# Gains of two norms: multiplied into the activations, or into the weights that follow them

## The reference, cut to what matters

```python
def rms_norm(x, g):
    y = x * rsqrt(mean(x * x, axis=-1) + 1e-6)
    return y * g                        # g: one gain per channel (1024)

xn = rms_norm(x, norm_mix[0])
x = x + moba_attention(xn, w_qkv, w_o)  # qkv = xn @ w_qkv, w_qkv 1024 x 3072
x = x + squared_relu_mlp(rms_norm(x, norm_mlp[0]), ...)
xn = rms_norm(x, norm_mix[1])
# group g of 256 channels: (trailing mean over 2, 4, 8 or 16 positions of xn) - xn,
# then a 256 x 256 map per group, then a scale per output channel
x = x + einsum(pooled, pool_w) * pool_scale
```

## Time and profile before

| | us |
|---|---|
| median of 3 runs (lowest to highest) | 1084.13 (1082.69 to 1084.5) |
| the profiled execution's own time | 1084.07 |
| its span, first to last instruction | 1082.1 |
| TensorE busy in the span | 1069.3 |
| VectorE busy | 740.3 |
| ScalarE busy | 561.1 |

### The profile page before, as it was taken

One profiled execution on the slowest core, in us unless ns is written; L12 is line 12 of the kernel. 1 busy time (PEld: TensorE's weight loads), 2 busy tenths in 40 slices (PEclk: granted clock), 3 DMA queues, 4 the chain that ended last, 5 costly groups with the idle time before them and its releaser, 6 DMA issues.

```text
span 1082.1 us, 15294 instructions
## 1 busy us (share of the span) xinstructions
PE 1069.3 (99%) x5812; PEld 909.6 (84%) x5812; DVE 740.3 (68%) x1044; ACT 561.1 (52%) x723; POOL 40.4 (4%) x60
## 2 busy tenths in 40 slices
PE   9999999999999999999999999999999999999997
PEld 6888888888888888889888888888889778888886
DVE  5756675655786656558897966666897879666665
ACT  5556443434455435346675554445654766444453
POOL 1000000000000000000000220000300300000000
PEclk9999999999999999999999999999999999999999
DMA  9953266465447465546633665657576324754651
GB/s 332 336 173 111 87 217 216 166 205 182 159 140 257 159 214 171 202 137 169 210 118 105 213 204 177 196 181 245 151 245 225 91 79 157 232 185 164 203 185 39
DMA packets 127163, 195.84 MB, mean 181 GB/s; under 512 B 6977, under 2 KB 97217, under 8 KB 126994
## 3 DMA queue, kind: packets, MB, share of 16 engines
q1 hardware_dynamic: 123904, 185.77, 51.7%
q0 software_dynamic: 3216, 9.51, 3.1%
q10 hardware_dynamic: 2, 0.00, 0.0%
HBM read 194.21 MB, written 1.05 MB: 180 GB/s over the span
## 4 chain that ended last, share of the span: by engine, by line
PE 94%; DVE 3%; ACT 1%; issue 1%; DMA 0%; DVEq 0%; ACTq 0%
PE ps L2108 26%; PE ps L2007 15%; PE ps L2009 15%; PE ps L2008 15%; PE ps L2111 13%; PE ps L2190 2%; PE ps L2229 1%; PE ps L2049 1%; PE ps L2192 1%; PE ps L2255 1%; PE ps L2640 1%; DVE act L1244 1%; PE ps L2288 1%; DVE wlo L1119 1%; PE ps L2469 0%
## 5 line engine op out<-in xcount | busy, mean ns | idle before, releaser
L2108 PE MATMUL ps<-act,whi 128*128 128x512 f32 x1200 | 425.0, 397 | 0.1
L1119 DVE TENSOR_TENSOR wlo<-raw,whi 128x2048 fp32r<-128x2048 f32 (+2 forms) x161 | 364.0, 2277 | 87.8 <-ACT whi L678 87.3
L2111 PE MATMUL ps<-act,wlo 128*128 128x256 f32 x1200 | 336.6, 281 | 0.0
L678 ACT ACTIVATE whi<-raw 128x2048 fp32r<-128x2048 f32 (+2 forms) x170 | 317.4, 1887 | 26.5 <-PE ps L2009 21.5
L2108 PEld LDWEIGHTS ps<-act,whi 128*128 128x128 f32 x1200 | 225.3, 188 | 54.4 <-issue 0.2
L2111 PEld LDWEIGHTS ps<-act,wlo 128*128 128x128 f32 x1200 | 226.7, 189 | 2.0
L2009 PE MATMUL ps<-whi,hlo 128*128 128x512 f32 x400 | 157.3, 393 | 0.0
L2008 PE MATMUL ps<-wlo,hhi 128*128 128x512 f32 x400 | 156.7, 392 | 0.0
L2007 PE MATMUL ps<-whi,hhi 128*128 128x512 f32 x400 | 156.2, 391 | 0.1
L2007 PE MATMUL ps<-whi,act 128*128 128x512 f32 (+2 forms) x286 | 112.4, 393 | 1.2 <-DVE act L1819 0.6
L2009 PE MATMUL ps<-whi,act 128*128 128x512 f32 (+2 forms) x286 | 108.0, 377 | 0.0
(11 more groups left out here) (231 smaller groups left out, 1155.6 us busy)
## 6 DMA issues: line engine op xcount, KB each, us to landing
raw<-mlp_w_up_in SPq DMA_DIRECT2D x32, 1024.0 KB, 6.2
raw<-mlp_w_down_in SPq DMA_DIRECT2D x32, 1024.0 KB, 4.9
raw<-ffn_w_gate_in SPq DMA_DIRECT2D x22, 1024.0 KB, 5.3
raw<-ffn_w_up_in SPq DMA_DIRECT2D x22, 1024.0 KB, 5.4
raw<-ffn_w_down_in SPq DMA_DIRECT2D x22, 1024.0 KB, 4.8
raw<-attn_w_qkv_in SPq DMA_DIRECT2D x10, 1024.0 KB, 8.9
raw<-w_kv_shared_in SPq DMA_DIRECT2D x8, 1024.0 KB, 5.3
raw<-attn_w_o_in SPq DMA_DIRECT2D x4, 1024.0 KB, 5.1
```

The source lines that it names most:

```text
L678: nc.scalar.activation(whi[:, s, 0:width], raw[:, s, 0:width], ACT.Copy).then_inc(hi_ready, 1)
L1119: nc.vector.tensor_tensor(wlo[:, s, 0:width], raw[:, s, 0:width], whi[:, s, 0:width].bitcast(F32), ALU.subtract).then_inc(lo_ready, 1)
L2108: nc.tensor.matmul(bank(b + f), lhsT=w[0][:, at:at + P], rhs=act[:, k, :, :].rearrange("p a t -> p (a t)"), start=k == 0, stop=False, skip ...
L2111: ins = nc.tensor.matmul(bank(b + f, 0, T), lhsT=w[1][:, at:at + P], rhs=act_hi[:, k, :], start=False, stop=k == KT - 1, skip_group_check= ...
```

## The change

The gains of both norms are loaded as 16 rows of 128 values (8 KB), turned once by TensorE to one column per block k, and copied to a small tile `gains`. `whi` and `wlo` of chunks 0 to 11 are made in four pieces of 512 columns, each with the column of its block as a per-partition scale. `pool_scale` and the second gain are multiplied into the pooling's weights in eight pieces of 256 columns. x itself is turned at the start, and x itself is multiplied by the band. `first_gained`, the spreading of the row, and `gained("mix1", ...)` are gone. The first quarter's dummies are six instead of three. Two rows leave the list `ROWS`, the order on VectorE at the start is another, and TensorE waits for x (`x_loaded`, `x_rest_loaded`, `x_ready`) where it waited for `xs_ready`.

```diff
-ROWS = ["mix0", "mlp0", "mix1", "pool_scale", "mlp1", "final", ...
+ROWS = ["mlp0", "pool_scale", "mlp1", "final", ...
@@ ScalarE
+            def hi_gained(s, k, gain):
+                return nc.scalar.activation(whi[:, s, k * HALF:(k + 1) * HALF], raw[:, s, k * HALF:(k + 1) * HALF],
+                                            ACT.Copy, scale=gains[:, gain:gain + 1])
             def hi_part(s, width, loaded, freed, gain=None):
...
+                for k in range(4):
+                    ins = hi_gained(s, k, gain + k)
+                ins.then_inc(hi_ready, 1)
...
-            act.dma_start(rows[0:1, 0, :], row_source["mix0"]...).then_inc(first_row_loaded, 16)
+            act.dma_start(junk[0:2 * KT, 0:P], a["norm_mix"].rearrange("l (k p) -> (l k) p", p=P))\
+               .then_inc(gains_loaded, 16)
             def hi_part_of(c, h, landed, done):
                 act.wait_ge(landed, 16)
-                nc.scalar.activation(whi[... h * D:(h + 1) * D], raw[...], ACT.Copy).then_inc(done, 1)
+                for k in (2 * h, 2 * h + 1):
+                    ins = hi_gained(SLOT[c], k, 4 * c + k)
+                ins.then_inc(done, 1)
             copy_turned("mix0", (0,))
+            act.wait_ge(gains_ready, 1)
             hi_part_of(0, 0, first_half_loaded, first_half_hi)
@@ VectorE
+            def lo_gained(s, k, gain):
+                cols = slice(k * HALF, (k + 1) * HALF)
+                return nc.vector.scalar_tensor_tensor(out=wlo[:, s, cols], in0=raw[:, s, cols],
+                                                      scalar=gains[:, gain:gain + 1],
+                                                      in1=whi[:, s, cols].bitcast(F32), op0=ALU.mult, op1=ALU.subtract)
...
-            dve.wait_ge(first_row_spread, 1)
+            dve.wait_ge(gains_turned, 1)
+            nc.vector.tensor_copy(gains[:, :], bank(3, 0, 2 * KT)).then_inc(gains_ready, 1)
             dve.wait_ge(x_loaded, 16)
             dve.sem_inc(x_ready, 2)
-            first_gained(0)
-            first_gained(1)
             split_turned("mix0", (0,))
+            dve.wait_ge(gains_ready, 1)
+            lo_part_of(0, 0, first_half_hi, 1, first_half_lo)
+            split_turned("mix0", (1,))
             dve.wait_ge(x_rest_loaded, 16)
             dve.sem_inc(x_ready, 2)
-            first_gained(2)
-            lo_part_of(0, 0, first_half_hi, 1, first_half_lo)
-            split_turned("mix0", (1,))
-            first_gained(3)
             split_turned("mix0", (2,))
             lo_part_of(0, 1, hi_ready, 1, lo_ready)
...
@@ scale_pool_weights
-                nc.vector.tensor_tensor(w, w, by_channel.broadcast_to([P, 4, 2, FC]), ALU.mult)\
-                    .then_inc(pool_weighted, 1)
+                for k in range(KT):
+                    w = raw[:, SLOT[c], k * FC:(k + 1) * FC]
+                    ins = nc.vector.scalar_tensor_tensor(out=w, in0=w, scalar=gains[:, KT + k:KT + k + 1],
+                                                         in1=row("pool_scale", k // 2 * FC, (k // 2 + 1) * FC),
+                                                         op0=ALU.mult, op1=ALU.mult)
+                ins.then_inc(pool_weighted, 1)
@@ pool_entry
                 add(0)
-                gained("mix1", 0)
                 add(1)
-                gained("mix1", 1)
                 variance(0)
                 newton(0).then_inc(scale_ready, 2)
                 add(2)
-                gained("mix1", 2)
                 add(3)
-                gained("mix1", 3)
                 release_row()
@@ TensorE
                 if name == "mix0" and 0 in parts:
-                    pe.wait_ge(ones_made, 1)
-                    pe.wait_ge(first_row_loaded, 16)
-                    for h in range(2):
-                        ins = nc.tensor.matmul(bank(2 + h), lhsT=scale_row[0:1, 0:P], ...)
-                    ins.then_inc(first_row_spread, 1)
                     pe.wait_ge(const_loaded, 16)
+                    pe.wait_ge(gains_loaded, 16)
+                    nc.tensor.transpose(bank(3, 0, 2 * KT), junk[0:2 * KT, 0:P], const[0:2 * KT, C_IDENT:C_IDENT + 2 * KT])\
+                        .then_inc(gains_turned, 1)
...
-                        for _ in range((3, 0, 3, 0)[p]):
+                        for _ in range((6, 0, 3, 0)[p]):
                             nc.tensor.matmul(bank(7, 0, P), lhsT=ident, rhs=ident, start=True, stop=True)
...
-                pe.wait_ge(xs_ready, 4 * XSR["mix1"] + 2 * t + 2)
+                pe.wait_ge(x_ready, 4 * XR["mix1"] + 2 * t + 2)
...
-                    ins = nc.tensor.matmul(o, lhsT=xs[:, t, kk * P:(kk + 1) * P], rhs=band[:, kk // 2, lo:hi],
+                    ins = nc.tensor.matmul(o, lhsT=x[:, t, kk * P:(kk + 1) * P], rhs=band[:, kk // 2, lo:hi],
```

More of the change, by code:

```diff
@@ L210, in two_blocks @@
         probs = sb("probs", [P, 4, 3 * P])
+        gains = sb("gains", [P, 2 * KT])
         probsT = junk[:, 0:6 * P].rearrange("p (a n) -> p a n", a=2)
@@ L610, in premix_rows @@
                 nc.gpsimd.tensor_scalar(both_rows[then], both_rows[then], -0.5, None, ALU.mult).then_inc(premixed, 1)
-            for name in ROWS[1:ROW["fpost0"] + 1]:
+            for name in ROWS[:ROW["fpost0"] + 1]:
                 load_row(name)
@@ L677, in hi_part @@
                     act.wait_ge(w_used, freed)
-                nc.scalar.activation(whi[:, s, 0:width], raw[:, s, 0:width], ACT.Copy).then_inc(hi_ready, 1)
+                if gain is None:
+                    nc.scalar.activation(whi[:, s, 0:width], raw[:, s, 0:width], ACT.Copy).then_inc(hi_ready, 1)
+                    return
+                for k in range(4):
+                    ins = hi_gained(s, k, gain + k)
+                ins.then_inc(hi_ready, 1)
             def hi_before(c):
@@ L1115, in link, with lo_part @@
                 dve.wait_ge(chain, links[0])
-            def lo_part(s, width, value):
-                dve.wait_ge(hi_ready, value)
-                nc.vector.tensor_tensor(wlo[:, s, 0:width], raw[:, s, 0:width], whi[:, s, 0:width].bitcast(F32),
-                                        ALU.subtract).then_inc(lo_ready, 1)
+            def lo_gained(s, k, gain):
[3 more added lines that the diff above has]
+                                                      in1=whi[:, s, cols].bitcast(F32), op0=ALU.mult, op1=ALU.subtract)
+            def lo_part(s, width, value, gain=None):
+                dve.wait_ge(hi_ready, value)
+                if gain is None:
+                    nc.vector.tensor_tensor(wlo[:, s, 0:width], raw[:, s, 0:width], whi[:, s, 0:width].bitcast(F32),
+                                            ALU.subtract).then_inc(lo_ready, 1)
+                    return
+                for k in range(4):
+                    ins = lo_gained(s, k, gain + k)
+                ins.then_inc(lo_ready, 1)
             def lo_before(c):
@@ L2031, in turn @@
                 if name == "mix0" and 0 in parts:
-                    pe.wait_ge(ones_made, 1)
-                    pe.wait_ge(first_row_loaded, 16)
-                    for h in range(2):
-                        ins = nc.tensor.matmul(bank(2 + h), lhsT=scale_row[0:1, 0:P],
-                                               rhs=rows[0:1, 0, h * HALF:(h + 1) * HALF], start=True, stop=True)
-                    ins.then_inc(first_row_spread, 1)
                     pe.wait_ge(const_loaded, 16)
+                    pe.wait_ge(gains_loaded, 16)
+                    nc.tensor.transpose(bank(3, 0, 2 * KT), junk[0:2 * KT, 0:P], const[0:2 * KT, C_IDENT:C_IDENT + 2 * KT])\
+                        .then_inc(gains_turned, 1)
                 for p in parts:
@@ L2045, in turn @@
                         keep_busy(BUSY[name][p], 7)
-                    pe.wait_ge(xs_ready, 4 * XSR[name] + p + 1)
+                    source_rows = x if name == "mix0" else xs
+                    if name == "mix0":
+                        pe.wait_ge((x_loaded, x_rest_loaded)[t], 16)
+                    else:
+                        pe.wait_ge(xs_ready, 4 * XSR[name] + p + 1)
                     k0, k1 = blocks[h]
```

46 lines of the change are left out of this document (16 added, 30 removed).

## The result

| | before | changed |
|---|---|---|
| median of 8 runs each (lowest to highest), us | 1084.66 (1082.69 to 1085.85) | 1088.88 (1087.88 to 1090.07) |
| own time of the profiled execution, and its span | 1084.07, 1082.1 | 1088.83, 1087.0 |
| mean granted clock in that span | 0.999 | 0.997 |

The medians are 4.2 us apart. The ratio, with the interval that goes with it, is 1.0043 [1.0034, 1.0052], or 3.7 to 5.6 us. The forecast was 1.75 more, and its range ended at 1088.2.

What follows compares the result with a forecast made beforehand. TensorE, 94% of the span, was taken as the bound. Chunk 4's +1.35, the pooling weights' +1.0 and the pooling entry's -0.6 made +1.75 on 1084.07: 1085.8, or 1085.9 against the median; 8-in-10 range 1084.0 to 1088.2.

Steps and rivals of the forecast that it cites:

- Chunk 4, forecast +1.35: Dearer `whi` and `wlo` pieces delay VectorE's copy; TensorE starts chunk 4 at 36.05, not 34.70, after a 3.0 us stop.
- the rival put at 0.2: TensorE's clock falls to half rate in the 3 us stop before chunk 4, costing 2 us: 1087.9; chance 0.2.
- The pooling: At the pooling, eight pieces on the weights cost +1.0 us, and dropping four multiplications at the entry gives -0.6.
- at TensorE (+1.0): Pooling's weights: eight pieces take 3.2 us instead of one instruction of 2.20, all on the path: +1.0.
- at the entry (-0.6): Pooling's entry: without four multiplications, tile 1's band products come 0.6 us sooner after the last down product.
- The early start is kept (0.07): Rival: at chunk 4 TensorE keeps most of the 1.7 us won at the start: 1082.1; chance 0.07.
- The gate: What holds chunk 4 back: SyncE's fifth 1 MB in a saturated queue, chunk 3 landing at 18.8.
- The cheap pieces (0.23): Rival: per-partition scales on the pieces cost nothing over immediate ones: +0.05, 1084.2; chance 0.23.
- Later chunks covered at 0: Behind chunk 4, each chunk's +0.60 on ScalarE and +0.46 on VectorE is covered by TensorE's 5.45 us.

Runs made afterwards that it cites:

- kernel with both holes filled: Changed kernel plus dummy products: five for three before x's third quarter, two before the first products, twelve in the stop before chunk 4; 1085.95 us, ratio 1.0022.
- the stop filled: Changed kernel plus 12 dummy products of 128 columns on TensorE between chunks 3 and 4; 1086.67 us, ratio 1.0028.
- The kernel with this part alone: Kernel before with only the pooling's part: eight pieces on its weights, four multiplications gone, band applied to x; 1084.94 us, ratio 1.0010.
- The last kernel: Kernel with the gaps of the start closed, plus chunk 5's `whi` and `wlo` before sine and cosine, factor product just ahead of the MLP's loop; 1082.67 us, ratio 0.9990.
- the kernel without pieces in these chunks: Kernel before with only the pooling's part of the change, start and chunks 0 to 11 as before; 1084.94 us, ratio 1.0010.
- kernel with the gaps of the start closed: Kernel with factors multiplied once, plus dummies: five for three before x's third quarter, two before the first products; 1084.93 us, ratio 1.0012.
- one piece: Changed kernel with `whi` and `wlo` of chunks 2 to 11 in one instruction each, without the first norm's gain; 1084.34 us, ratio 1.0009.
- reordered: Changed kernel with chunk 4's `whi` and `wlo` before squares, root and angles, chunks 4 and 5 in banks 6 and 7; 1084.72 us, ratio 1.0005.
- factors multiplied once: Reordered kernel with gain x pool_scale multiplied once before the first MLP, so the pooling's weights take one instruction; 1085.80 us, ratio 1.0017.

## Why the prediction was right or wrong

- **The direction, and the place.** Slower, by a stop at chunk 4 released by VectorE's copy, and by the pooling's weights: so it came. The first product started at 11.19, not 10.6: the half chunk landed at 8.18, not 7.87, and the steps behind it took 0.3 more.
- **Chunk 4, forecast +1.35, measured 36.45 - 34.70 = +1.75.** The chain was right link by link, and its prices too: what is over is mostly that the weights landed later in this execution, the first half chunk at 8.18 and chunk 3 at 19.10, where the profile of the kernel before has 7.90 and 18.79. (Over the profiles of all kernels chunk 3 lands at 18.73 to 19.14.) Less these 0.31, VectorE's mean stands at 24.07 (forecast 24.11), its copy at 35.24 (35.21) and chunk 4 at 36.14 (36.05). In the kernel with both holes filled the landing was at 18.73, and chunk 4 started at 36.06. That this is so near is in part luck, because the forecast saw only one of two routes to the mean, the one by chunk 3's landing. The other goes from the turn of x's last quarter (14.25) through its copy (14.72) and `whi` of chunks 1 and 2 to `wlo` of chunk 2 at 19.02; VectorE's eight pieces from there would have ended within 0.1 of the same time. By this route TensorE's own start matters: with the turn 1.4 late, chunk 4 came 1.34 late (the stop filled).
- **The step that failed is the rival put at 0.2, and at 0 in the sum: TensorE's clock in the 3 us stop.** The stop was 2.70 long, and behind it the granted clock was 0.55 and 0.59. In none of the eight executions of the changed kernel was the mean clock above 0.998. The rival priced the fall at 2 us for 4 us of low level; measured is 1.5 for 3.1 to 3.3 us (by the distances of the products in two executions, and by 12.65 - 11.16 with the gaps filled). The argument against it, that 1.64 us of idleness in the pooling had left the next matmuls fast, said nothing on a stop nearly twice as long, as the text itself noted; a stop longer than any shown should have made this rival the middle of the forecast. In the terms of the sum: 1.75 at chunk 4, 1.5 for the fall, 0.25 for the first products behind a stop (0.26 with the clock held) and 0.32 at the pooling are +3.8, and 1084.1 + 3.8 = 1087.9 to a measured 1088.9.
- **The range** ended at 1088.2 because it reached to this rival alone; the rival's own spread, with chunk 4 at the high end, lay outside.
- **The pooling.** Eight pieces 3.18 us (3.2 forecast), +0.96 at TensorE (+1.0), -0.64 at the entry (-0.6), +0.32 in sum (+0.4): right. The kernel with this part alone repeats it.
- **The early start is kept (0.07).** It was not. The last kernel shows what it takes: chunks 4 and 5 converted early, another pair of banks, and no fall of the clock in the start. The gate was as stated, chunk 3's landing; a later TensorE, though, pushes chunk 4 back.
- **The cheap pieces (0.23).** False: 0.61 and 0.67 apart. By the Trainium skill (ScalarE: Activation LUTs, "What ACT_TABLE_LOAD costs") a 512-column instruction with one per-partition operand is an estimated 0.71 long and 0.61 apart; the trace agrees, with 0.71 and 0.61.
- **Later chunks covered at 0**: confirmed. From chunk 4 on the 48 products of the kernel with both holes filled take 47.22 - 36.06 = 11.16, 0.26 above 48 x 0.227, and from the heads to the band the changed kernel takes the same 259.17 as the kernel without pieces in these chunks. In the kernel with the gaps of the start closed, where TensorE is ahead, chunk 5 does stop it, for 0.63 us.

What stays open: the two profiled spans are 4.9 us apart, 1087.0 - 1082.1. 3.8 of it stands in the rows up to the band, and 1.1 in the 778 us behind it, for which no run gives a cause; the medians are 4.2 apart. Also open is which of the executions with gaps of around 1 us at the start lose the clock.

## What to carry to other kernels

A wait that is added to the bounding engine costs its length and then, if it is long, half rate behind it: price it with the clock, or fill it with dummy matmuls in the same edit. Making the engine start earlier was worth nothing until the chain of the other engines up to its next dependence was also shorter, while a later start was passed on in full; walk that chain instruction by instruction, at the price of pieces. Many small instructions on the helpers are a longer latency even where their engines have time to spare.

## What the runs showed of the hardware that was not expected

- TensorE's granted clock fell after far shorter gaps than the stop, where it had only just risen. Two gaps of 1.22 and 0.91 (one piece), 1.26 and 0.92 (reordered), 0.77 and 0.94 (stop filled) and 0.83 and 0.83 (factors multiplied once) were followed by 0.43 between products for six to eight distances. Gaps of 0.72 and 0.86 in the first profile of the changed kernel and 1.62 and 0.80 in the second were not. With two dummies in the second gap, which left 0.5 of it, none of three profiles had the fall. So length alone does not decide it, and these runs do not say what does.
- The fall need not stand right behind the gap: in the second profile of the changed kernel four products ran at full pace behind 2.78 us of idleness before the slow ones came.
- The page's clock row showed the top digit everywhere: a fall of 3.3 us weighs 6% of a slice of 27 us. Only stretches of 2 us, or the distance between matmuls, show it. At the very start even the stretches don't: the kernel before has 1.00 from 6 to 8 us, where four turns took 0.87 against 0.44 later.
- The timeline joins instructions that stand close, and so it hides short waits: ten ScalarE pieces seemed 0.64 apart and were 0.61 apart with one wait for a landing.
